# Order of the expert matmuls and release of the weight ring in a mixture-of-experts block

## The reference, cut to what matters

```python
def expert_rows(args):
    xb, e = args
    return (jax.nn.silu(xb @ w1[e]) * (xb @ w3[e])) @ w2[e]
...
out = jnp.zeros((t, d), h.dtype).at[row_tok].add(yb * row_w[:, None])
```

## Time and profile before

| | us |
|---|---|
| median of three runs | 1793.96 |
| the profiled execution's own time | 1790.49 |
| its span in the profile | 1788.8 |
| PE busy | 1720.6 (96% of the span) |
| PE busy with the up matmuls, L2022 | 457.1 |
| PE busy with the down matmuls, L2049 | 210.8 |
| weights and inputs read from HBM | 534 MB |

### The profile page before, as it was taken

One profiled execution on the slowest core, in us unless ns is written; L12 is line 12 of the kernel. 1 busy time (PEld: TensorE's weight loads), 2 busy tenths in 40 slices (PEclk: granted clock), 3 DMA queues, 4 the chain that ended last, 5 costly groups with the idle time before them and its releaser, 6 DMA issues.

```text
span 1788.8 us, 22386 instructions
## 1 busy us (share of the span) xinstructions
PE 1720.6 (96%) x9480; PEld 1136.1 (64%) x9480; DVE 683.1 (38%) x743; ACT 429.6 (24%) x462; POOL 170.0 (10%) x223
## 2 busy tenths in 40 slices
PE   8999999999999999999999999999999999999997
PEld 7998989988788888888544444344444433443442
DVE  5357777555744645543122211221122202220222
ACT  6343445325523433343000000000000000000002
POOL 5000042310141100000000000000000000000001
PEclk9999999999999999999999999999999999999998
DMA  8454445423533455658999999999999999999997
GB/s 257 152 165 164 146 138 189 141 96 118 189 115 98 148 188 184 217 182 344 367 428 428 427 428 428 428 429 428 429 429 428 428 429 428 428 428 429 428 426 289
DMA packets 95329, 537.51 MB, mean 300 GB/s; under 512 B 5836, under 2 KB 5900, under 8 KB 70044
## 3 DMA queue, kind: packets, MB, share of 16 engines
q1 hardware_dynamic: 94672, 535.85, 75.5%
q0 software_dynamic: 592, 0.69, 0.3%
HBM read 534.42 MB, written 2.10 MB: 300 GB/s over the span
## 4 chain that ended last, share of the span: by engine, by line
PE 72%; DMA 22%; DVE 2%; ACT 2%; issue 1%; POOL 0%; SPq 0%; DVEq 0%; ACTq 0%
DMA arena<-in_w 22%; PE psum L2022 13%; PE psum L2049 9%; PE psum L1556 9%; PE psum L1558 9%; PE psum L1557 9%; PE psum L1943 4%; PE psum L1575 3%; PE psum L1576 3%; PE psum L1577 3%; PE psum L1782 1%; PE psum L1774 1%; PE psum L2067 1%; PE psum L2066 1%; PE psum L1984 1%
## 5 line engine op out<-in xcount | busy, mean ns | idle before, releaser
L2022 PE MATMUL psum<-arena 128*64 128x512 f32 x2048 | 457.1, 603 | 38.7 <-DMA arena<-in_w 37.9
L2022 PEld LDWEIGHTS psum<-arena 128*64 128x64 f32 x2048 | 147.8, 139 | 337.1 <-issue 286.6
L1056 DVE TENSOR_TENSOR w_lo<-arena,w_hi 128x2048 fp32r<-128x2048 f32 x119 | 274.4, 2309 | 188.0 <-ACT w_hi L728 178.0
L728 ACT ACTIVATE w_hi<-arena 128x2048 fp32r<-128x2048 f32 x119 | 227.3, 1912 | 267.4 <-PE psum L1558 191.3
L1556 PE MATMUL psum<-w_hi,hT_hi 128*128 128x512 f32 x568 | 228.5, 402 | 0.1
L1557 PE MATMUL psum<-w_lo,hT_hi 128*128 128x512 f32 x568 | 225.6, 397 | 0.0
L1558 PE MATMUL psum<-w_hi,hT_lo 128*128 128x512 f32 x568 | 225.6, 397 | 0.0
L2049 PE MATMUL psum<-arena 128*64 128x512 f32 x960 | 210.8, 594 | 4.5 <-DMA arena<-in_w 4.5
L2049 PEld LDWEIGHTS psum<-arena 128*64 128x64 f32 x960 | 67.0, 137 | 137.0 <-issue 124.4
L1575 PE MATMUL psum<-hT_hi,w_hi 128*128 128x256 f32 x512 | 145.7, 285 | 0.0
L1577 PE MATMUL psum<-hT_hi,w_lo 128*128 128x256 f32 x512 | 144.6, 282 | 0.0
(11 more groups left out here) (368 smaller groups left out, 1547.9 us busy)
## 6 DMA issues: line engine op xcount, KB each, us to landing
arena<-in_w SPq DMA_DIRECT2D x184, 2048.0 KB, 26.6
arena<-in_w_in SPq DMA_DIRECT2D x87, 1024.0 KB, 5.0
arena<-in_w_out SPq DMA_DIRECT2D x16, 1024.0 KB, 5.0
arena<-in_w SPq DMA_DIRECT2D x14, 1024.0 KB, 20.9
arena<-in_w_oa SPq DMA_DIRECT2D x8, 1024.0 KB, 5.0
arena<-in_w_ob SPq DMA_DIRECT2D x8, 1024.0 KB, 5.1
arena<-in_x SPq DMA_DIRECT2D x4, 1024.0 KB, 7.3
arena<-in_w SPq DMA_DIRECT2D x4, 512.0 KB, 15.9
```

The lines of the kernel that those rows point to most:

```text
L728: nc.scalar.activation(w_hi[x % NSPLIT], ringA[:, x % RING_A, :], ACT.Copy).then_inc(sem("w_hi"), 1)
L1056: tt(w_lo[x % RING_A], ringA[:, x % RING_A, :], w_hi[x % NSPLIT].bitcast(F32), ALU.subtract)\
L2022: i = mm(bank(w)[e * CAP:(e + 1) * CAP, :], xeT[:, k, e * CAP:(e + 1) * CAP], src[e][:, (k % 8) * CB:(k % 8 + 1) * CB], start=(k == 0), st ...
```

## The change

Three things. PE takes the experts one after the other within each half matrix: all 8 pieces of e0 (16 instructions of the trace), then all 8 of e1; the same in the down stage, where e1's second half goes bank by bank. Each slot has a semaphore of its own, `slotM0` to `slotM7`, and is released alone. The four 1 MB loads of the first down matrix are gone: these slots are loaded like all others, whole, after the release of the slot. In the last pair the second half of w3 and the down stage keep their order with the experts innermost.

```diff
-            for half in range(2):
-                for e in range(2):
-                    if half:
-                        sp.wait_ge(sem("slotM_free"), RING_M + e + 1)
-                    else:
-                        wait(sp, ("first_part", 2))
-                    sp.dma_start(ringM[e][:, half * D:(half + 1) * D], w2_v[e, :, half * D:(half + 1) * D])\
-                        .then_inc(sem("slotM0" if half else "part_in"), 16)
-            load_pair(0, 0, 0, RING_M + 2, PER_PAIR)
+            load_pair(0, 0, 0, RING_M, PER_PAIR)
...
-                    pe.wait_ge(sem(f"slotM{at % RING_M // 2}"), it * 96 + 32 * (at // RING_M + 1))
-                    return [ringM[at % RING_M + e] for e in range(2)]
+                    pe.wait_ge(sem(f"slotM{at % RING_M}"), it * 48 + 16 * (at // RING_M + 1))
+                    return ringM[at % RING_M]
...
+                    for half in range(2):
+                        order = [(e, q) for e in range(2) for q in (2 * half, 2 * half + 1)]
+                        if not more and w and half:
+                            order = [(e, q) for q in (2, 3) for e in range(2)]
+                        for e, q in order:
+                            if first and w == 0:
+                                if e == 0:
+                                    pe.wait_ge(sem("xe"), q + 1)
+                                elif half == 0:
+                                    gather(n, 2 + q, first=True)
+                            if q % 2 == 0:
+                                arrived(4 * w + 2 * half + e)
...
+                            for k in range(CT * q, CT * q + CT):
...
+                            if q % 2:
+                                i.then_inc(sem("slotM_free"), 1)
...
+                for half in range(2):
+                    for e in range(2):
+                        src = arrived(8 + 2 * half + e)
+                        order = [(t, k) for t in range(2) for k in range(NC)]
+                        if half and e:
+                            order = [(t, k) for k in range(NC) for t in range(2)]
```

More of the change, by code:

```diff
@@ L479, in load_pair @@
                     sp.dma_start(ringM[slot], v[bass.ds(pair * 2 + e, 1), :, q * MS:(q + 1) * MS]
-                                 .rearrange("a p n -> (a p) n")).then_inc(sem(f"slotM{slot // 2}"), 16)
+                                 .rearrange("a p n -> (a p) n")).then_inc(sem(f"slotM{slot}"), 16)
             wait(sp, ("mT", NC))
@@ L515, in last_slot @@
                                more_rounds * (PAIRS * PER_PAIR) + ((PAIRS - 1) * PER_PAIR + j + 1))
-                return ringM[slot], f"slotM{slot // 2}"
+                return ringM[slot], f"slotM{slot}"
             for piece in range(2):
@@ L1977, in last_down @@
                     else:
-                        src = arrived(8 + 2 * half)
+                        src = [arrived(8 + 2 * half + e) for e in range(2)]
                     for t in range(2):
@@ L2010, in expert_pair @@
                         pe.wait_ge(sem("comb"), n + 1)
[L2011 to L2021, removed]
-                                i = mm(bank(w)[e * CAP:(e + 1) * CAP, :], xeT[:, k, e * CAP:(e + 1) * CAP],
[L2023 to L2027, removed]
+                    for half in range(2):
[10 more added lines that the diff above has]
+                                arrived(4 * w + 2 * half + e)
+                            elif not more and w and half and e == 0:
+                                wait(pe, ("part_in", 48))
+                            src = ringM[(PER_PAIR * u + 4 * w + 2 * half + e) % RING_M]
+                            for k in range(CT * q, CT * q + CT):
+                                i = mm(bank(w)[e * CAP:(e + 1) * CAP, :], xeT[:, k, e * CAP:(e + 1) * CAP],
+                                       src[:, (k % 8) * CB:(k % 8 + 1) * CB], start=(k == 0), stop=(k == KT - 1))
+                            if q % 2:
+                                i.then_inc(sem("slotM_free"), 1)
@@ L2041, in expert_pair @@
                     return last_down(n, u, arrived)
[L2042 to L2048, removed]
+                for half in range(2):
[4 more added lines that the diff above has]
+                            order = [(t, k) for k in range(NC) for t in range(2)]
+                        for odd, k in order:
+                            t = 2 * half + odd
                             i = mm(bank(4 + k)[e * CAP:(e + 1) * CAP, :],
                                    aT[:, t * P + e * CAP:t * P + (e + 1) * CAP],
-                                   src[e][:, (t % 2) * D + k * CB:(t % 2) * D + (k + 1) * CB],
+                                   src[:, odd * D + k * CB:odd * D + (k + 1) * CB],
                                    start=(t == 0), stop=(t == FT - 1))
[L2053 to L2056, removed]
+                            if e and t == FT - 1 and k < NC - 1:
+                                i.then_inc(sem("down"), 1)
+                        i.then_inc(sem("slotM_free"), 1)
                 for k in range(NC):
```

## The result

The changed kernel takes 2120.4 us (median of six runs, 2115.9 to 2121.9), the kernel before 1794.5 us in the same series. The ratio is 1.1815, with a 95% interval of 1.1798 to 1.1833: slower by 18%. The profiled execution of the changed kernel took 2117.2 us, with a span of 2115.5 us.

What follows compares the result with a forecast made beforehand. Weights bound before, PE after: first pair to 942.5 us, 14 pairs x 78.0 and last pair 74.9 give span 2109.4, plus 5.2, about 2115 us. Two overtaken matmuls would give about 2180 us, four 2050.

Steps and rivals of the forecast that it cites:

- What bounds the kernel: Weights at 428 GB/s, 58.8 us a pair, bound it before; PE needs 53.9 us, leaving 4.9 us of slack.
- the next run starts when three matmuls of the run before are left: Up and down blocks: a run of 16 costs 12 steps, the last 16; 56 more steps, 24.1 us a pair.
- The queues behind it: PE's instruction queue: some 28 places handed on in order to a short queue of five or six entries per half.
- A pair of 78.0 us: Middle pairs with all weights there: PE's 53.9 us plus 24.1 us, above the weights' 58.8 us, so PE becomes the bound.
- The first pair: First pair, where gathers use the full array: 28.1 us more, from 59.6 to 87.7 us.
- The last pair: Last pair: w1 +8.6 us, first half of w3 +5.2 us, DMA waits gone; from 63.8 to 74.9 us.
- Semaphores: Six more waits in a pair on PE, 51 ns each: nothing; 5 us if the sequencer's lead fails to cover them.
- The half loads: First down matrix: one slot, 4.9 us, moved later; hidden behind PE at no cost, 5.4 us if PE's cover is gone.
- the first rival: Free overlap: halves run apart at any run length, PE stays at 53.9 us, late slot paid; 1799.4 us, no chance stated.
- No overlap over a change of run: Rival: each run waits for the end of the one before, 41.3 us more a pair; about 2376 us, no chance stated.
- Free overlap: Rival: halves run apart however long the runs, weights still bound, late slot paid; 1799.4 us, no chance stated.
- DMA at about 320 GB/s: Sign in the profile after the change, expected with pairs of some 78 us and no PE wait for DMA.

Runs made afterwards that it cites:

- e3: Changed kernel with the two experts switched after every four matmuls (runs of 8 instructions) instead of eight; 1813.3 us, 1.0098 of the kernel before.
- e10: Changed kernel with the two experts switched after every two matmuls (runs of 4 instructions); 1791.4 us, 0.9995 of the kernel before.
- e6: Changed kernel with mixed run lengths in the up matrices: five then three matmuls per expert in w1, six then two in w3; 1983.7 us, one run.
- e2: Kernel before with only the order by expert, in all pairs but the first; old semaphores and half loads stay; 2092.2 us, ratio 1.1668.
- e5: Changed kernel with every second half matrix of an up matrix in reversed expert order, giving runs of 16, 32, 32, 32, 16 instructions; 2192.0 us, one run.
- e7: Changed kernel with each down matmul cut into two of 256 columns, up matmuls unchanged; 2163.0 us, one run.
- e9: Changed kernel with down matmuls, except the last pair's, reading the upper 16 bits as bf16, one instruction each; 1848.5 us, one run.
- e1: As a run, not the expert: changed kernel with the experts alternated innermost again, per-slot semaphores and missing half loads kept; 1793.9 us, 1.0002 of the kernel before.
- e4: Kernel before with only the half loads removed, slots 0 and 1 of the first down matrix loaded whole; 1793.8 us, ratio 0.9998.

## Why the prediction was right, point by point

- **What bounds the kernel.** Right. The weights before; PE after, with 4.9 us of slack in a pair as the limit: e3, whose pair takes 58.55 us of PE (4.7 more, within the slack), never waits for a DMA, and is the first to lose time.
- **The two instructions side by side are e0's and e1's, and the next run starts when three matmuls of the run before are left.** Right, to the size. In the changed kernel the starts of single instructions show it: e1's first starts at 948.677, 6 ns behind the thirteenth of e0's sixteen (948.671), and e0's last three start after it. Foreseen were 100 steps for an up block and 52 for a down block. A step of one expert alone is 0.429 us, (7.08 - 3.65) / 8 by the rows of 16 and of 8 in the first pair, and what a block takes over its steps is 0.21 us (7.08 - 16 x 0.429). With these two numbers all lengths of run agree:

| instructions in a run | up block, us | changes of expert | steps by the rule | steps measured |
|---|---|---|---|---|
| 2 (before) | 27.69 | 63 | 64 | 64.1 |
| 4 (e10) | 27.74 | 31 | 64 | 64.2 |
| 8 (e3) | 30.25 | 15 | 68 | 70.0 |
| 10, 6, 12, 4 (e6) | 34.95 | 15 | 80 (81 expected) | 81.0 |
| 16 (after, e2) | 43.53 | 7 | 100 | 101.0 |
| 16, 32, 32, 32, 16 (e5) | 48.51 | 4 | 112 | 112.6 |

  What is left over the rule goes with the changes between long runs: 2.0, 1.0 and 0.6 steps for 15, 7 and 4 of them (e3, after, e5), 0.13 to 0.15 of a step each. The down block's 22.70 us are 52.4 steps for 52, with 3 changes. The starts in the changed kernel show it too: each run starts 5.206 us after the one before it, 12 steps and 0.057 us. Its first instruction starts 6 ns behind the other expert's, and takes 0.480 us until its second starts, where all others take 0.429. The rule of four steps left this out.
- **The queues behind it** (one in order, with a short one for each half) were a picture that gave the rule. The runs show its consequence, a fixed four instructions (e7, e9), and exclude a share of the run and a span of time. That I came to three from two counts that differ by two instructions (18 and 20), with a picture that no run shows, is in part luck. The runs don't show the picture: a search through a window of entries from the oldest one would give the same lengths, and no run was made that tells the two apart.
- **A pair of 78.0 us.** 78.47 measured. The step of 0.43 us was right (0.429). What the sum lacked is the 0.057 us of each change of expert: 53.9 + 56 x 0.429 + 10 x 0.057 = 78.5. Over fourteen pairs the 0.47 us make 6.6. The span is 6.1 over the forecast (2115.5 against 2109.4): besides these 6.6 the first pair starts 1.2 us later than in the profile before, and the first and the last pair are 0.2 and 1.5 us under what I had put.
- **The first pair,** 87.7 us foreseen, took 87.5 (943.47 - 855.98), and the first half of its first up matrix 18.0 us with its gathers. (Its second gather stands between e1's two pieces, as the sum has it; only the first stands between e0 and e1, other than the section on the change says.) In the second half I let e1 end at step 33; with runs of 8, 16 and 16 the rule gives 4 + 12 + 16 = 32, and the block of 40 took 14.06 us, 32.3 steps. That is 0.4 us too much in the sum, and the changes that it lacks are 0.5: the two nearly cancel. **The last pair,** 74.9 foreseen, took 73.4:

```profile
2042.10 40.21 PE L2019 MATMUL psum<-arena 128*64 128x512 f32 x128
2083.08 0.75 PE L2028 MATMUL psum<-arena 128*128 128x128 f32 x4 [0.78 <-DVE arena L1477]
2084.71 7.09 PE L1976 MATMUL psum<-arena 128*64 128x512 f32 x32 [0.88 <-ACT arena L977]
```

  The down block's first 32 instructions are down from 8.78 us to 7.09, as foreseen; the up blocks took 40.21, where the 27.9 of the earlier trace rows and my 13.8 more gave 41.7. I had counted the ends of w1 and of the first half of w3 as unshared, 4 steps each, but the blocks follow one another without a break. And the second half of w3 doesn't keep the old order, as the section on the change and I had it: its loop is by quarter, expert, piece, so it runs in groups of four matmuls of one expert, as in e3. By the rule six runs of 16 and four of 8 are 6 x 12 + 3 x 4 + 8 = 92 steps, and with nine changes 40.2 us.
- **Semaphores: nothing.** Right, by e1, which keeps them all and is at 1.0002.
- **The half loads: hidden in the forecast.** Right there, but the price that I gave them without cover, 5.4 us, is not borne out: e1 and e4, in which the weights bound, measure none. The failed step is "one slot, 4.9 us, is moved later". I had seen that before the change the transfers slacken right after the half loads, and still counted the delay as if the engines had been full from then on. In e4 the late loads are still under way when the next slots come free, and fill the place of that slack. Both runs release slots 0 and 1 at one time, though. The changed kernel's own order gives slot 0 free at 863.1 and slot 1 only at 874.2, by the issues of SP; what that would cost without PE's cover no run shows, and so it stays open whether the first rival would have been 1799.4 us or nearer to 1794.
- **No overlap over a change of run** (2376 us): excluded by the shared steps at each change. It is what follows from the rule of TensorE: Matmul & The Clock Gate, What overlaps and what doesn't, in the Trainium skill, that matmuls start strictly in program order. In the changed kernel e1's first matmul starts while three earlier ones of e0 have not started. **Free overlap,** to which Key Properties of TensorEngine Tiling in the Trainium skill leads when it is read alone, holds up to runs of four instructions (27.74 us against 27.69) and not beyond.
- **The total.** 2115 forecast, 2120.4 measured; part of the closeness is that the terms above miss in both directions. DMA at about 320 GB/s was named as a sign, and it is 320.

## What to carry to other kernels

Where two streams of matmuls use different halves of the array's columns, interleave them finely in the program: here groups of up to four instructions of one stream (two fp32 matmuls) cost nothing, runs of eight cost four steps wherever a block starts afresh, and of every longer run all but the first four and the last four instructions had the array to themselves. PE's busy share doesn't show this; count the weight loads, or the instructions, in a fixed stretch and compare with the count of a stretch that is known to overlap. When pricing a transfer that starts later, look at whether the queue would have run dry before the next release anyway: the late load then fills that hole, and the hole has only moved.

## What the hardware showed that I had not expected

- The rule holds to the instruction. Fourteen pairs of 78.47 us, the same 43.53 us in three different kernels, and a second expert that starts 6 ns behind the fourth instruction from the end, for 512 columns of fp32, for 256, and for bf16. Each change between long runs adds 0.057 us with fp32 and 512 columns.
- Cutting matmuls into shorter ones makes an ordering of this kind worse: 25.42 us for 22.70 (e7).
- A bf16 matmul of 512 columns took a step of 0.227 us, an fp32 one two instructions of 0.429 us each, so the fp32 one costs 3.8 times as much.
